# A product of zeros between the halves of each up unit of the feed-forward pairs

## What is computed

```python
h = h + 0.5 * _swiglu(_rmsnorm(h, ffn1_norm[layer]), ffn1_w_in[layer], ffn1_w_out[layer])
...
h = h + 0.5 * _swiglu(_rmsnorm(h, ffn2_norm[layer]), ffn2_w_in[layer], ffn2_w_out[layer])

def _swiglu(x, w_in, w_out):
    a, b = jnp.split(x @ w_in, 2, axis=-1)
    return (jax.nn.silu(a) * b) @ w_out
```

## Time and profile before

| | |
|---|---|
| two executions | 1837.8 and 1830.72 us, median 1834.26 |
| the profiled execution | 1838.21 us |
| its span | 1836.2 us, mean granted TensorE clock 0.99 |
| TensorE busy | 1790.6 us, 98% |
| VectorE, ScalarE, GpSimd busy | 66%, 47%, 34% |
| DMA | 336.58 MB, 183 GB/s on average |

### The profile page before, as it was taken

One profiled execution on the slowest core, in us unless ns is written; L12 is line 12 of the kernel. 1 busy time (PEld: TensorE's weight loads), 2 busy tenths in 40 slices (PEclk: granted clock), 3 DMA queues, 4 the chain that ended last, 5 costly groups with the idle time before them and its releaser, 6 DMA issues.

```text
span 1836.2 us, 35458 instructions
## 1 busy us (share of the span) xinstructions
PE 1790.6 (98%) x15337; PEld 1744.7 (95%) x15341; DVE 1203.6 (66%) x1378; ACT 868.6 (47%) x1102; POOL 624.2 (34%) x752
## 2 busy tenths in 40 slices
PE   8999999999999999999999899999999999999999
PEld 7999999999999999999998789999999998789999
DVE  7977667666664766676665965556655567756654
ACT  5254445544444544464344354334554446665442
POOL 6977881586753788010001810000000003420000
PEclk9999999999999999999999999999999999799999
DMA  6456665454444556658555345664446653015552
GB/s 264 176 205 220 225 212 220 161 179 172 161 172 150 175 213 218 223 203 320 187 198 188 121 165 190 223 218 173 161 149 205 219 192 114 24 54 191 194 190 109
DMA packets 53799, 336.58 MB, mean 183 GB/s; under 512 B 7899, under 2 KB 11020, under 8 KB 16908
## 3 DMA queue, kind: packets, MB, share of 16 engines
q1 hardware_dynamic: 46272, 300.00, 45.6%
q10 hardware_dynamic: 3276, 19.64, 2.9%
q0 software_dynamic: 4096, 14.68, 2.3%
HBM read 318.54 MB, written 15.75 MB: 182 GB/s over the span
## 4 chain that ended last, share of the span: by engine, by line
PE 82%; DVE 8%; POOL 4%; ACT 4%; issue 2%; DMA 1%; SPq 0%; ACTq 0%; POOLq 0%; DVEq 0%
PE psum L480 25%; PE psum L482 24%; PE psum L481 24%; DVE w_lo L1984 3%; ACT w_hi L1181 2%; POOL swap L1901 1%; DVE both L1991 1%; PE psum L980 1%; PE psum L1076 1%; ACT both L1181 1%; DVE yc L2322 1%; DVE h L1997 1%; PE psum L1093 1%; PE psum L797 1%; PE psum L1110 1%
## 5 line engine op out<-in xcount | busy, mean ns | idle before, releaser
L480 PE MATMUL psum<-both,w_hi 128*128 128x256 f32 x3584 | 1007.9, 281 | 24.7 <-DVE both L1991 11.2
L482 PE MATMUL psum<-both,w_lo 128*128 128x256 f32 x3584 | 997.7, 278 | 0.0
L481 PE MATMUL psum<-both,w_hi 128*128 128x256 f32 x3584 | 997.7, 278 | 0.0
L1984 DVE TENSOR_TENSOR w_lo<-raw,w_hi 128x2048 fp32r<-128x2048 f32 x277 | 655.9, 2369 | 272.9 <-ACT w_hi L1181 271.7
L1181 ACT ACTIVATE w_hi<-raw 128x2048 fp32r<-128x2048 f32 (+1 forms) x281 | 535.9, 1909 | 556.2 <-PE psum L482 544.8
L480 PEld LDWEIGHTS psum<-both,w_hi 128*128 128x128 f32 x3584 | 677.1, 189 | 31.5 <-issue 11.7
L481 PEld LDWEIGHTS psum<-both,w_hi 128*128 128x128 f32 x3584 | 679.6, 190 | 0.5 <-issue 0.2
L482 PEld LDWEIGHTS psum<-both,w_lo 128*128 128x128 f32 x3584 | 677.0, 189 | 0.0
L1733 POOL TENSOR_TENSOR ssum<-sq 128x512 f32<-128x512 f32 x11 | 16.8, 1526 | 715.0 <-ACT sq L1205 715.0
L480 PE MATMUL psum<-hid_hi,w_hi 128*128 128x256 f32 x640 | 178.2, 278 | 0.5 <-ACT vcmp L1181 0.5
L481 PE MATMUL psum<-hid_lo,w_hi 128*128 128x256 f32 x640 | 177.3, 277 | 0.0
(11 more groups left out here) (393 smaller groups left out, 2067.2 us busy)
## 6 DMA issues: line engine op xcount, KB each, us to landing
raw<-in_weights SPq DMA_DIRECT2D x279, 1024.0 KB, 4.8
table<-tables ACTq DMA_DIRECT2D x8, 1792.0 KB, 9.8
tables<-st POOLq DMA_DIRECT2D x16, 512.0 KB, 4.9
tables<-st POOLq DMA_DIRECT2D x8, 256.0 KB, 4.7
tables<-turns POOLq DMA_DIRECT2D x8, 256.0 KB, 4.4
w<-in_cmp_w ACTq DMA_DIRECT2D x4, 512.0 KB, 6.5
tbl<-in_cmp_w ACTq DMA_DIRECT2D x4, 512.0 KB, 5.3
tbl<-bias_v SPq DMA_DIRECT2D x128, 16.0 KB, 4.8
```

What stands on the lines that cost most here:

```text
L480: nc.tensor.matmul(out, a_hi, b_hi, start=start, stop=False, skip_group_check=True)
L481: nc.tensor.matmul(out, a_hi, b_lo, start=False, stop=False, skip_group_check=True)
L482: return nc.tensor.matmul(out, a_lo, b_hi, start=False, stop=stop, skip_group_check=True)
L1984: tt(w_lo[:, g % RING], raw[:, g % RING], w_hi[:, g % RING].bitcast(F32), ALU.subtract).then_inc(sem["lo_ready"], 1)
```

## The change

In the loop of `ffn` both up units get a `mid`: one product of the 128x128 zeros with `count` columns of zeros, added to the unit's own bank between its halves. The count comes from a table of 20 widths, two per k, the same in all four stages: A takes 256, 260, 264, 268, 240, 244, 248, 252, 128, 192 for k = 0 to 9, B 258, 262, 266, 270, 242, 246, 250, 254, 130, 224. The result is not altered by it. The first A and B units, the down units and all else stay as they were.

```diff
+WIDTHS = (256, 258, 260, 262, 264, 266, 268, 270, 240, 242, 244, 246, 248, 250, 252, 254, 128, 130, 192, 224)
...
+            def nudge(bank, count):
+
+                nc.tensor.matmul(bank[:, 0:count], zero[:, 0:P], zero[:, 0:count], start=False, stop=False,
+                                 skip_group_check=True)
+
...
                 for k in range(0, FFN_PAIRS - 1):
                     pe.wait_ge(sem["a_scaled"], FFN_PAIRS * f + k + 1)
-                    up_unit(g + 2, k, x, A_BANK)
+                    up_unit(g + 2, k, x, A_BANK, mid=lambda: nudge(A_BANK, WIDTHS[2 * k % len(WIDTHS)]))
                     if side is not None and k == 0:
                         side[2]()
                     pe.wait_ge(sem["b_gated"], FFN_PAIRS * f + k + 1)
-                    up_unit(g + 3, k, x, B_BANK)
+                    up_unit(g + 3, k, x, B_BANK, mid=lambda: nudge(B_BANK, WIDTHS[(2 * k + 1) % len(WIDTHS)]))
```

## The result

The changed kernel took 1866.09 us (median of 1865.5 and 1866.67), beside 1834.26 before: a ratio of 1.0176, 95% interval 1.0123 to 1.0228, so slower by 1.2 to 2.3%. The profiled execution is the one of 1866.67 us, its span 1864.6: 28.4 more than before.

What follows compares the result with a forecast made beforehand. TensorE, busy without waits in the feed-forward stages, was taken as the bound. Onto the profiled 1838.2 us came 9.2 direct price, 2.8 for more long steps and 1.1 settling, +13.1: 1851 us, range 1840 to 1864.

Steps and rivals of the forecast that it cites:

- TensorE bounds, and everything added is paid in full: In the four feed-forward stages TensorE never waits, so whatever is added to its queue lengthens the span by its full price.
- Two stable steps, 113.3 and 117.8 ns, and a new entry at each added product: Feed-forward streams keep a step of 113 or 118 ns per product; each of 80 added products can change it behind itself.
- The share at the long step, 0.36: Share of the stream products behind added ones running at the slower step: 0.36 x 25.5 = 9.2 us, 2.8 more than now.
- The direct price, 115 ns: In the middle of each up unit, the added product itself costs 115 ns: 80 x 0.115 = 9.2 us.
- The upper bound: Highest price for the added products, if a weight load is left uncovered at each: 80 x 0.205 = 16.4 us.
- rival D: Weight load uncovered on one side of each added product, 7.2 us more: 1858.5 us with the forecast share; chance 0.08.
- Settling, 1.1 us: Streams that end short behind an added product first make four steps of about 119 ns: 22 ns for each of 51.
- C: Rival: all or nearly all streams behind the added products run at the long step, 1866.5 us; chance 0.06.
- A: Rival: every stream behind an added product falls to the short step, 1842.8 us; chance 0.20.
- B: Rival: added products leave the stream's step unchanged, 1847.4 us with `ffn1` long, 1840.7 with it short; chance 0.18.
- E: Rival: not slower; added products in the up units cost only 3.1 us, all streams become short: 1834.9 us; chance 0.05.
- The answer of a width is the same in all stages: Sign to check: if width decides, the step behind an added product of a given width is the same in all stages.

## Why the prediction was wrong, point by point

- *TensorE bounds, and everything added is paid in full*: right. No wait came or went in the stages, the granted clock stayed at 1.00.
- *Two stable steps, 113.3 and 117.8 ns, and a new entry at each added product*: right, and it is where the time went: 16.1 of 28.4 us. That a stream keeps its step "past every change of bank, weight slot and operand" holds for the tiles as this kernel places them; with `hid_hi` and `hid_lo` 64 bytes further on, the down units that read them (all 23 in the streams) went to 116.7 ns.
- *The share at the long step, 0.36*: this step failed. It took the 16 widths of 240 and more as products that cover the next load, with the entries of the earlier trace rows as their kind. They don't: behind every width from 128 to 270 the second split product starts 199 to 206 ns after the first, as behind the narrow products of the earlier trace rows. The class was chosen by the width, where the row to look at was the load: a float32 load has a step of 112 ns, and 264 columns at 0.42 ns each (the wide products above) make 111. Taken for all 80, the share of the earlier trace rows's kind, 39 of 52, would have made 0.75 x 25.5 = 19.1 less 6.4, so 12.7 in place of 2.8 us, and 1861 in all, inside the range. The measured share was 0.87, 16.1 us. The count of other entries was no law either: 264 columns start the second product 202 or 203 ns behind the first, the kind that had ended long 39 times of 52, and all 80 ended short.
- *The direct price, 115 ns*: it was 126 to 130; 10.2 us instead of 9.2. Bounds right, value a little low. The upper bound did not come as a price: a distance of 0.20 us does stand behind each added product, which was named as a sign of rival D, but the one before it is only 0.04.
- *Settling, 1.1 us*: smaller, about 0.3, as only 12 entries ended short.
- *Between the stages*: 2.1 us that the sum had not; by the scatter outside the streams it could have been several us either way.
- *The rivals*: C, nearly all long, named 1866.5 us, and the profiled execution took 1866.67. Its mechanism is what happened, but that it meets to 0.2 us is luck: the long steps cost 3.0 us less than its 19.1, the added products 1.0 more, and 2.1 lie outside. It had a chance of 0.06, because it was weighed by the same wrong class. A is what 264 columns do, 1846; B fell with the first added product of `ffn0`, which came in short and left long. D and E fell by the 126 ns, against their 205 and 38 to 40. The chance of being over 2% slower, 0.035, is more than its parts give, a fifth of D's 0.08 and the 0.01 for the unseen.
- *The answer of a width is the same in all stages*: put as a test; it held to the extent of the table with the incoming step as a further condition, with 260 columns but for 1 of 80, and not for the fp32r product, where the same width out of a long stream gave 27 long and 24 short.

## What to carry to other kernels

A TensorE that is busy 100% at full clock can still run its stream at two speeds: compare the count of products per window between stages that do the same work, before looking for waits. Before a small product is put into a dense stream, look at the load behind it and at what the rows show behind others like it, and judge the product by the longer of its columns and that load; products on operands that the stream itself uses cost their step and nothing else here, one per half unit, written to columns that are started anew. A change that only moves tiles can change the step as well: look at the units that read them before the change is given the blame. And where a small edit slows a kernel by more than its own instructions, count steps on both sides of it.

## What the runs showed of the hardware that was not expected

- Streams of fp32r products of 256 columns run at 113.3 or at 117.8 ns per product and kept either over 1500 products. The entry decides, by small differences: out of a short stream 264 columns ended short and 266 long; 504 and 512 short and 508 long.
- A zero bf16 product between them costs 126 to 130 ns at any width from 128 to 264, then 0.42 ns for each further column (235 at 512).
- An fp32r product with an operand from the tile of zeros disturbs a stream for a few steps (118, 119, 116, 114 ns), on the stream's own operands it doesn't; either operand is enough. Whether it is the tile's place or the zeros in it is not shown.
- Moving a tile by 64 bytes took all 23 down units that read it from 113.3 to 116.7 ns per product. What in the place does it stays open: only one other place was tried.
- Two zero operands threw 29 of 29 short streams to the long step when the product wrote the finished half from the old place, and none of 78 when it wrote the other half from the new one. Which of the two changes did it is open.
- Why the long step is 4.4 ns longer is open as well. In it a product's record lasts 280 ns or so against 276, and no run here looks further down.
